# A recurrent head's output norm one head later, and its level factors right behind their spans: the third layer of a four-layer fp32 kernel

## The reference

```python
qf = silu(q); f = lb + (1 - lb) * sigmoid(fz)
logf = log(maximum(f, TINY)); k = (1 - lb) * sigmoid(-fz)
# per chunk of 64 tokens, state S
b = cumsum(logf)
att[t, s] = sum_k q[t, k] * k[s, k] * exp(b[t, k] - b[s, k])      # s <= t
o = att @ v + (q * exp(b)) @ S
o = o * rsqrt(mean(o * o) + 1e-6) * gain        # per head
ya = o * silu(g)
```

## Time and profile before

| | us |
|---|---|
| median of 3 runs | 2698.28 (2698.16 to 2698.64) |
| the profiled execution | 2698.26 |
| its span, first to last instruction | 2696.6 |
| PE busy | 2645.9 (98%) |
| DVE busy | 1700.1 (63%) |
| the stage of the change | about 1077 to 1625 of the span |

### The profile page before, as it was taken

How to read it: one execution, slowest core, us unless ns; L and a number is a source line. 1 busy time by engine, 2 the same in 40 slices (tenths; PEclk the granted TensorE clock), 3 DMA queues, 4 the chain that set the end, 5 groups by cost and what they waited for, 6 DMA issues and landing times.

```text
span 2696.6 us, 54722 instructions
## 1 busy us (share of the span) xinstructions
PE 2645.9 (98%) x20724; PEld 2521.9 (94%) x20724; DVE 1700.1 (63%) x3640; ACT 579.3 (21%) x1397; POOL 310.9 (12%) x473
## 2 busy tenths in 40 slices
PE   8999999999999999999999999999999999999997
PEld 7888889999999999899999999999999999999997
DVE  7667666565555566777777762656555566778855
ACT  3221221110011012322222221112112011434411
POOL 0011110010010000322222220112211000000000
PEclk9999999999999999999999999999999999999999
DMA  6434433444444444333333325433333444444442
GB/s 248 142 132 140 139 126 126 166 160 161 159 163 159 156 156 165 135 133 129 124 124 124 124 95 194 157 126 126 140 142 126 173 171 164 161 166 164 187 157 109
DMA packets 63757, 401.03 MB, mean 149 GB/s; under 512 B 6816, under 2 KB 13488, under 8 KB 17456
## 3 DMA queue, kind: packets, MB, share of 16 engines
q1 hardware_dynamic: 62992, 397.62, 40.9%
q0 software_dynamic: 672, 2.11, 0.5%
HBM read 397.60 MB, written 2.11 MB: 148 GB/s over the span
## 4 chain that ended last, share of the span: by engine, by line
PE 86%; DVE 9%; issue 3%; ACT 1%; DMA 1%; DVEq 0%; SPq 0%; ACTq 0%
PE psum L588 57%; PE psum L534 12%; PE psum L543 2%; PE psum L856 2%; DVE wide_b L2109 1%; PE psum L1042 1%; PE psum L662 1%; PE psum L761 1%; DVE w L2073 1%; PE psum L563 1%; DVE wide_a L474 1%; PE psum L669 1%; PE psum L1051 1%; DVE ring L1627 1%; DVE wide_c L1626 1%
## 5 line engine op out<-in xcount | busy, mean ns | idle before, releaser
L588 PE MATMUL psum<-h,ring 128*128 128x128 f32 x4384 | 524.5, 275 | 0.4 <-DVE near L1660 0.4
L588 PEld LDWEIGHTS psum<-h,ring 128*128 128x128 f32 x4384 | 507.9, 192 | 1.7 <-DVE near L1660 0.6
L588 PE MATMUL psum<-mix,ring 128*128 128x128 f32 x3994 | 477.8, 276 | 0.6 <-DVE near L1660 0.3
L588 PEld LDWEIGHTS psum<-mix,ring 128*128 128x128 f32 x3994 | 461.5, 192 | 1.6 <-DVE near L1660 1.5
L534 PE MATMUL psum<-h,ring 128*128 128x256 f32 x2016 | 454.1, 382 | 0.0
L534 PEld LDWEIGHTS psum<-h,ring 128*128 128x128 f32 x2016 | 376.5, 190 | 59.5 <-issue 12.7
L1667 DVE TENSOR_TENSOR near<-psum,near 128x128 f32<-128x128 f32 x128 | 37.4, 292 | 365.9 <-PE psum L588 365.9
L543 PE MATMUL psum<-ring,h 128*128 128x128 f32 x1536 | 175.4, 275 | 0.0
L543 PEld LDWEIGHTS psum<-ring,h 128*128 128x128 f32 x1536 | 174.1, 192 | 0.5
L1627 DVE TENSOR_TENSOR ring<-ring 128x1024 f32<-128x1024 f32 x128 | 157.4, 1230 | 0.0
L1110 ACT ACTIVATE w<-psum 128x128 f32<-128x128 f32 x87 | 24.1, 277 | 540.5 <-PE psum L588 540.5
(11 more groups left out here) (447 smaller groups left out, 3908.2 us busy)
## 6 DMA issues: line engine op xcount, KB each, us to landing
ring<-w_out SPq DMA_DIRECT2D x80, 1024.0 KB, 5.1
ring<-w_odd SPq DMA_DIRECT2D x64, 1024.0 KB, 4.9
ring<-w_hgrn SPq DMA_DIRECT2D x64, 1024.0 KB, 4.9
ring<-w_even SPq DMA_DIRECT2D x48, 1024.0 KB, 4.9
ring<-w_nsa SPq DMA_DIRECT2D x48, 1024.0 KB, 6.0
ring<-w_rg SPq DMA_DIRECT2D x40, 1024.0 KB, 5.7
ring<-w_cmp_in SPq DMA_DIRECT2D x8, 1024.0 KB, 4.9
ring<-w_rgg SPq DMA_DIRECT2D x10, 512.0 KB, 7.4
```

What stands on the lines that cost most here:

```text
L588: mm = pe.matmul(dst, stationary, moving, start=new and j == 0, stop=new and j == kh - 1, skip_group_check=not new)
```

## The change

The 16 heads' arithmetic is the same. What moves:

- **factors**: `low_decays(i)` stands right behind the spans on DVE, ahead of the forms; its memset goes to an own step `state(i)` that waits for `attend(i-1)`; ACT's exponential of levels 0 to 3 becomes two instructions of two levels.
- **output norm**: `output_norm` and `mixed` of head i-2 (not i-1) stand among the level copies of turn i, `turn_output` of head i-2 behind run 5, ahead of `attend`.
- **third combination**: `b12 - b22` is no more in `three_forms` but a step `new_block` of its own at the turn's end, signal `block_made`, which PE awaits ahead of run 4.
- **gate**: `output_gate(i)` stands at the end of turn i and writes straight into `mix`.
- **head 0 and 1**: the norm's ones-matmuls come behind block 10 (not 4) of the first product; two of the four `sums` go into head 1, which is now written out apart; ACT's gate tanh of head 0 comes before the higher exponentials.

```diff
-            def unscaled(stationary, dst, x_raw, raw_from, between=None):
+            def unscaled(stationary, dst, x_raw, raw_from, between=None, place=4):
...
-                    if between is not None and k == 4:
+                    if between is not None and k == place:
...
             def far_keys(j):
 
-                pe.wait_ge(h_mixed, after(j))
+                pe.wait_ge(h_mixed, after(j - 1))
...
-            def turn_output(j):
-
+            def turn_output(j, more=True):
+
+                pe.wait_ge(att_ready, after(j + 2 if more else j + 1))
                 pe.wait_ge(ho_norm, after(j + 1))
...
+            def levels_and_block(j):
+
+                levels(j, (5, 6))
+                pe.wait_ge(block_made, after(j + 1))
+
+            def last_level(j):
+
+                levels(j, (7,))
+                far_keys(j)
+
+            def output_and_attend(j, second):
+
+                if not second:
+                    turn_output(j - 1)
+                attend(j)
+
+            def head(i, first, second=False):
...
-                    unscaled(lambda k: tile(hgrn, 0, k), bank[0][:, 0:T], raw_last, 2 * KT, lambda: norm_pair(1))
+                    unscaled(lambda k: tile(hgrn, 0, k), bank[0][:, 0:T], raw_last, 2 * KT, lambda: norm_pair(1), 10)
...
-                                    (3, lambda: levels(j, (5, 6))), (4, lambda: (levels(j, (7,)), far_keys(j))),
-                                    (5, lambda: attend(j))))
+                                    (3, lambda: levels_and_block(j)), (4, lambda: last_level(j)),
+                                    (5, lambda: output_and_attend(j, second))))
...
-                product(hgrn, i, 3, bank[1], 0, 8)
-                if not first:
-                    turn_output(i - 1)
-                product(hgrn, i, 3, bank[1], 8, KT)
+                product(hgrn, i, 3, bank[1])
 
             head(0, True)
-            with pe.Fori(1, HEADS) as i:
+            head(1, False, True)
+            with pe.Fori(2, HEADS) as i:
                 head(i, False)
...
             product(cmp_in, 0, 1, bank[1], 0, 4)
+            turn_output(last - 1)
             attend(last)
             product(cmp_in, 0, 1, bank[1], 4, KT)
-            turn_output(last)
+            turn_output(last, False)
...
-                s.wait_ge(span_low, after(i + 1))
-                s.activation(wide_b[:, 0:4, :], wide_a[:, 0:4, :], ACT.Exp).then_inc(decay_low, 1)
+                for n in range(2):
+                    s.wait_ge(span_low, after(2 * i + n + 1))
+                    s.activation(wide_b[:, 2 * n:2 * n + 2, :], wide_a[:, 2 * n:2 * n + 2, :], ACT.Exp)\
+                        .then_inc(decay_low, 1)
+                if first:
+                    gate_of(i)
                 s.wait_ge(span_ready, after(12 * i + 12))
                 s.activation(wide_b[:, 4:8, :], wide_a[:, 4:8, :], ACT.Exp).then_inc(decay_ready, 1)
-                gate_of(i)
+                if not first:
+                    gate_of(i)
...
             def low_decays(i):
 
-                st.mark(v.memset(small[:, :], 0.0))
                 st.settle()
                 v.wait_ge(hq_used, after(i + 1))
-                v.wait_ge(decay_low, after(i + 1))
                 for lv in range(4):
+                    if lv % 2 == 0:
+                        v.wait_ge(decay_low, after(2 * i + lv // 2 + 1))
...
             def output_gate(j):
 
-                v.wait_ge(h_mixed, after(j))
                 v.wait_ge(hg_tanh, after(j + 1))
-                v.scalar_tensor_tensor(gz[:, :], gate[:, :], 1.0, bank[1][:, 0:T], ALU.add, ALU.mult)\
+                v.scalar_tensor_tensor(head_of(j), gate[:, :], 1.0, bank[1][:, 0:T], ALU.add, ALU.mult)\
...
+            def two_forms(i, first=False):
...
+                (b11, b21, b12, b22), (t2, t1, t4) = pieces(fast_h, 0)[0]
+                then(v.tensor_tensor(t1, b12, b11, ALU.subtract))
+                v.tensor_tensor(t2, b22, t1, ALU.subtract).then_inc(forms_made, 1)
+
+            def new_block():
+
+                (b11, b21, b12, b22), _ = pieces(fast_h, 0)[0]
+                v.tensor_tensor(b12, b12, b22, ALU.subtract).then_inc(block_made, 1)
+
+            def state(i):
+
+                v.wait_ge(ho_ready, after(i))
+                st.mark(v.memset(small[:, :], 0.0))
+
+            def head(i, second, last):
 
                 keep_levels(i - 1, (0, 1, 2))
+                if second:
+                    sums(sums_h, h[:, 0:8, :], h[:, 8:16, :], 44, (2,))
+                    new_block()
                 first_sum(fast_h, i, 0)
                 keep_levels(i - 1, (3, 4))
+                if second:
+                    sums(sums_h, h[:, 0:8, :], h[:, 8:16, :], 44, (3,))
+                else:
+                    output_norm(i - 2)
+                keep_levels(i - 1, (5, 6))
                 fourth_form(fast_h, i, 0)
-                keep_levels(i - 1, (5, 6))
                 two_sums(fast_h, i, 0, fq)
                 keep_levels(i - 1, (7,))
+                if not second:
+                    mixed(i - 2)
                 fourth_sum(fast_h, i, 0, fq)
                 forget_in(i)
+                state(i)
                 fifth_sum(fast_h, i, 0, fq)
                 keys_of(i)
                 queries_of(i)
                 sums_of_logs(i)
-                output_norm(i - 1)
+                low_decays(i)
                 if not last:
-                    three_forms(fast_h, i + 1, 0)
-                low_decays(i)
-                mixed(i - 1)
+                    two_forms(i + 1)
+                output_gate(i)
+                if not last:
+                    new_block()
...
             sums_of_logs(0)
+            low_decays(0)
             v.wait_ge(h_ready, after(3 * KT))
-            sums(sums_h, h[:, 0:8, :], h[:, 8:16, :], 44)
-            three_forms(fast_h, 1, 0, True)
-            low_decays(0)
...
+            sums(sums_h, h[:, 0:8, :], h[:, 8:16, :], 44, (0, 1))
+            two_forms(1, True)
+            output_gate(0)
```

More of the change, by code:

```diff
@@ L414, in program @@
         span_low, decay_low = signal("span_low"), signal("decay_low")
+        block_made = signal("block_made")
         lv_ready, lv_used, att_far, att_ready = (signal(n) for n in ("lv_ready", "lv_used", "att_far", "att_ready"))
@@ L882, in turn_output @@
                 mm.then_inc(ht_ready, 1)
-            def head(i, first):
+            def levels_and_block(j):
[9 more added lines that the diff above has]
+            def head(i, first, second=False):
                 f_pair = fast_h.number(i, 0)
@@ L2092, in sums_of_logs @@
                     for n, ins in enumerate(spans(v, lv)):
-                        if (lv, n) != (3, 1):
+                        if (lv % 2, n) != (1, 1):
                             st.mark(ins)
@@ L2136, in output_norm @@
                 v.wait_ge(ho_guess, after(j + 1))
+                v.wait_ge(h_mixed, after(j))
                 st.mark(v.tensor_copy(cur[:, 3:4], lbt[:, 3, ds(j, 1)]))
@@ L2151, in mixed @@
                 v.wait_ge(ht_ready, after(j + 1))
-                v.scalar_tensor_tensor(mix[:, ds(j, 1), :].rearrange("p a t -> p (a t)"), bank[4][:, 0:T],
-                                       cur[:, 3:4], gz[:, :], ALU.mult, ALU.mult).then_inc(h_mixed, 1)
-            def head(i, last):
-                output_gate(i - 1)
+                v.scalar_tensor_tensor(head_of(j), bank[4][:, 0:T], cur[:, 3:4], head_of(j), ALU.mult, ALU.mult)\
+                    .then_inc(h_mixed, 1)
+            def two_forms(i, first=False):
+                for n in range(2):
+                    v.wait_ge(landed[hgrn.loads[n].slot], hgrn.loads[n].land0 + i * hgrn.loads[n].land_per)
+                if not first:
+                    v.wait_ge(used, done(hgrn, i - 1, 3))
+                else:
+                    v.wait_ge(used, hgrn.scratch_free[3])
+                (b11, b21, b12, b22), (t2, t1, t4) = pieces(fast_h, 0)[0]
[8 more added lines that the diff above has]
+            def head(i, second, last):
                 keep_levels(i - 1, (0, 1, 2))
+                if second:
+                    sums(sums_h, h[:, 0:8, :], h[:, 8:16, :], 44, (2,))
+                    new_block()
                 first_sum(fast_h, i, 0)
                 keep_levels(i - 1, (3, 4))
+                if second:
+                    sums(sums_h, h[:, 0:8, :], h[:, 8:16, :], 44, (3,))
+                else:
+                    output_norm(i - 2)
+                keep_levels(i - 1, (5, 6))
                 fourth_form(fast_h, i, 0)
-                keep_levels(i - 1, (5, 6))
                 two_sums(fast_h, i, 0, fq)
                 keep_levels(i - 1, (7,))
+                if not second:
+                    mixed(i - 2)
                 fourth_sum(fast_h, i, 0, fq)
                 forget_in(i)
+                state(i)
                 fifth_sum(fast_h, i, 0, fq)
@@ L2184, in _ @@
             sums_of_logs(0)
+            low_decays(0)
             v.wait_ge(h_ready, after(3 * KT))
```

(20 more changed lines are left out.)

2 lines of the change are left out of this document (added).

## The result

The changed kernel takes 2667.32 us (median of 4 runs, 2666.90 to 2668.10) against 2698.23 for the kernel before in the same rounds (2698.16 to 2698.64): 30.9 us off, a ratio of 0.9885 [0.9868, 0.9903]. The profiled execution took 2667.21, 31.05 less than the one before.

A forecast was written before the change was run, and what follows sets the result against it. PE, busy 98%, bounds the kernel; its gaps are nearly all one wait for DVE's low factors at the first level product. Gains of 24.2 (turns) plus 4.2 (heads 0 and 1), 28.4 off 2698.26, give 2669.9 us; range 2667.5 to 2678.

The forecast's parts named there:

- The turns: Steady turns of the loop: the wait at L859 goes, 32.99 to 31.26 us each, 14 x 1.73 = 24.2 us.
- new waits, 2.3: Head 1's pair: DVE's list makes PE wait anew, 1.0 at run 2, 1.0 at `attend`, 0.3 at the last but one level.
- The three losses: Heads 0 and 1 before: norm's matmul about 1.0, late L859 3.78, slow PE clock 1.7 us; together 6.5 gained.
- a wait of 1.0: Run 2 of head 1's pair: DVE's list ends at 1110.1, PE is there at about 1109.1, 1.0 us.
- another 1.0: Head 1's pair: DVE's eighth copy comes at 1120.9 against `attend` at 1120.0, 1.0 us.
- The last 0.3: Head 1's pair: a new wait of 0.3 us at the last but one level.
- The transposes, the memset, the tail: Transposes and memset moved at no cost, 0.5 and 0.3 us without cover; tail's two added transposes cancel, zero in sum.
- The first: Loop: the norm is too much among the copies, `attend` waits; 0.5 per turn, 7.5 us back, 2677.4; chance 0.09.
- The second: Loop: PE waits for POOL's factors, held up by DVE operations; 16.5 us back, 2686; chance 0.06.
- The third: Loop: L859's wait stays, the factors hanging on something besides DVE's order; 2694 to 2698 us; chance 0.02.
- the fourth rival: Loop: slower, DVE's middle stretch becoming the bound; 3.5 us longer would give 2706 us; chance 0.02.

The follow-up runs named there:

- fourth: Changed kernel with the low factors behind the two forms again in the loop (heads 2 and on): 2667.74 us.
- fifth: Changed kernel with DVE's old turn end (three forms, factors, gate), the norm staying one head later: 2668.78 us.
- tenth experiment: Kernel before with one added wait, POOL's high factors waiting for DVE's low ones: 2673.86 us, ratio 0.9909.
- experiment one: Changed kernel with the third combination directly behind the two forms, ahead of the gate, also in heads 0 and 1: 2668.84 us.
- three: Changed kernel with one exponential of 1024 columns for levels 0 to 3, behind all the spans: 2671.70 us.
- twelve: Changed kernel with all four sums in head 0 again, none left over for head 1's pair: 2671.04 us.
- the eight memsets: Changed kernel with eight memsets of an unused tile, each waited for, behind the output norm among the level copies: 2692.55 us.
- seventh experiment: Kernel before with the low factors right behind the spans, ahead of the output norm and the forms: 2766.99 us, ratio 1.0252.
- sixth: Kernel before with the low factors behind the output norm but ahead of the three forms in the loop: 2677.15 us.
- eighth experiment: Changed kernel with three memsets of an unused tile, each waited for, behind the output norm among the level copies: 2668.23 us.

## Why the prediction was off by a little, step by step

**The turns: right.** 31.26 predicted, 31.24 measured; 24.2 predicted, 24.5 measured. The wait went, and nothing took its place in the loop. The sizes inside were pessimistic: the factors took 1.85 and not 3.3, since beside them POOL was not at its eight products but at its spans. Neither this nor any spare was needed to the full, since 1.73 us had to be found, and the factors ended 5.3 ahead of their due time. That is why three partial edits (fourth, fifth and tenth experiment) give the turns back just as well.

**Head 0 and 1: the step that failed is "new waits, 2.3".** The three losses were sized well: 6.5 predicted, and the traces give 6.6. The norm's place is 1.2 of them (the first product and the norm take 8.95 us before, 7.77 with the change). The late L859 and the slow clock are 5.4 (11.25 us from run 1 to run 3 of head 1's pair, where 5.81 is the time without a wait). The opening is shorter by 6.14. So the new waits came to about 0.5 us and not 2.3, and nearly all of that stands at another place, for another engine.

At run 2 I had a wait of 1.0, and there is none: DVE's gate ended at 1108.44 and run 2 started at 1108.56, against 1110.1 and 1109.1 in the prediction. Some 0.54 of either difference is only the earlier start of the stage in this execution. With that taken off, the end of the spans and run 2 lie where I had them. What was mis-sized is DVE's list between them, 7.0 us and not 8.05: most of it the factors, 1.8 up to the next row where I took 2.7 (a mean between alone and beside POOL's products), and a little the sums and forms, at 1.15 to 1.25.

At `attend` I had another 1.0: the last copy at 1120.9 against 1120.0. It ended at 1117.82, against `attend` at 1118.59. About 1.1 of that comes from the same list; of the rest, 1.4, no more can be said than that the pair's list was also taken too long, since the prediction doesn't give its entries.

The last 0.3, "at the last but one level", did come, but I had put it down to DVE's copies. The level product at 1113.36 is the fifth position, which waits for POOL's high factors, and these ended at 1113.30: in head 0 they took 6.25 us beside DVE's copies, sums and combination. That wait of 0.3, with the slower first matmuls behind it, is 0.4 us. In experiment one, where PE comes 1.2 later to this place, it is gone.

I had the mechanism of the waits at run 2: experiments one, three and twelve put them there, as soon as DVE gets 1.2 us more to do. I paid for a collision that had not been reached.

**The range** had its low end where those 2.3 us vanish, 2667.6. 1.8 of them did, with 0.3 more in the turns, 0.1 more in the three losses, and 0.54 from the stage's start. That last part is chance: with it taken off, the profiled execution would have been 2667.75, inside the range, whose low end left nothing for a scatter of 1.7 us over this study. The distance to the forecast, 2.6 us, is for the most part not chance but the 1.8.

**The transposes, the memset, the tail: right**, at nothing, with 0.3 us for one wait in the last head.

**Rivals.** The first's price is confirmed by the eight memsets, and its condition wasn't met. The second did not occur in the loop: in the turn shown POOL's products ended 1.65 behind L860, while PE wants them 5.8 behind. In head 1 it did, once and for 0.3 us, at the very product that the rival names. Its rule deserves a closer look, because it spoke for the change and I had put it down as a danger. The traces show a DVE product at twice its time beside POOL's two-input products (537 to 286 ns), and about its own time (312 ns) beside POOL's one-input operations of 64 columns; there POOL is the one that waits (its L1542 took 1.46 us beside a form of 1024 columns, and 0.65 in the fourth experiment, where the forms were over). The Trainium skill, page "SBUF — State Buffer", section "Who interferes with whom", says that a VectorE instruction with two SBUF inputs contends with a GpSimd instruction that reads SBUF, for a pair of ports that is an exclusive lock. These runs agree, and add that an operation beside longer ones of the other engine loses the more: POOL's operations of 64 columns went from about 0.5 us to 1.5 beside DVE's of 1024 (1.2 us), DVE's products to twice their time beside POOL's, and POOL's products from 3.37 for eight to 5.35. The third and the fourth rival did not occur, and the seventh experiment shows a way to be slower which the list did not have: the same reordering without the move of the transposes.

**Left open.** A stall of 3.6 us ahead of the first level product stands in four profiled executions. In one, the kernel before, 3.41 us at half clock went with it; in the sixth, seventh and tenth experiment 6.83. No run tells what decides. The openings there were 51.5 to 51.6 us and not 50.54, so the execution from which the prediction was read was the mild case, and the change may save some 7.1 us there rather than 6.14 in others. No variant here was faster than the change: the fourth and the eighth experiment agree with it within their scatter. No experiment keeps POOL apart from DVE in the changed kernel's head 0, so that it would gain the 0.4 us isn't shown.

## What to carry to other kernels

When an engine sits at 98% and its idle time is one wait, repeated each turn, the gain is that wait and no more, and the cheapest edit that covers it is enough: try a wait that keeps two engines' two-input operations apart before reordering a program. In the first turns of a loop, add up the waiting engine's list with durations taken beside the neighbours that it will have, not those that it had. Read the waits of the weight loads beside those of PE: the one for POOL in head 1 stands only there. If a stretch is tight, keep each piece of it that looks worthless in steady state: stalls of 2.4 us and more cost 0.4 to 1 times their own length again in clock in these runs.

## What the runs showed of the hardware

- An activation's table load of 1.28 us began only when the semaphore wait of its activation was met. A smaller first activation whose input is early pulls it forward; here that was worth 4.4 us with what followed, and it had been costed at 0.2 us of loss.
- PE's clock and an idle stretch: after 0.7, 1.2 and 1.5 us it stayed at 2.4 GHz; with 2.43 and 2.65 us it went to 1.2 for 3.41 us, from 0.4 us behind the restart in the first case and from the restart in the second; with 3.09 us (in the loop) and 5.81 for 6.83 us, beginning 0.9 and 2.5 us ahead of the restart; with 3.6 for 3.41 in one execution and 6.83 in three. Half of the part in which PE worked was lost each time.
- With the same program in front, the stage's first matmul scattered by 1.7 us between executions. The first 32 matmuls of the kernel alone, at the clock's first rise, took 9.91 us in the profile before and 8.95 in the one after, and the next product began at 17.61 and 17.11: that is where 0.50 of the 0.54 us come from.
